# Merging eight masked score levels one at a time in the odd mixer of a two-layer block pair

## What is computed

```python
G = jnp.cumsum(gc, axis=2)
decay = jnp.exp(jnp.where(tri, G[:, :, :, None, :] - G[:, :, None, :, :], -jnp.inf))
scores = jnp.einsum('bhik,bhjk,bhijk->bhij', qc, kc, decay)
o = jnp.einsum('bhij,bhjv->bhiv', scores, vc) + jnp.einsum('bhik,bhkv->bhiv', qc * jnp.exp(G), s)
```

## Time and profile before

| | |
|---|---|
| Median of 3 runs | 3082.21 us (3080.93 to 3082.76) |
| The profiled execution | 3080.94 us, its span 3079.1 us |
| TensorE's share of the span | 97% |
| VectorE's share of the span | 24% |
| The odd mixer's units | about 943 to 1260 us into the span |

### The profile page before, as it was taken

The page is one execution under the profiler, slowest core; times in us unless marked ns, Lnnn a source line. Parts: engine busy times, 40 slices in busy tenths (PEclk is TensorE's granted clock), DMA queues, the critical chain, the costliest instruction groups (busy, mean ns, idle before and its releaser), DMA issues.

```text
span 3079.1 us, 41222 instructions
## 1 busy us (share of the span) xinstructions
PE 2976.5 (97%) x17952; PEld 1702.2 (55%) x17952; DVE 732.1 (24%) x1737; ACT 399.4 (13%) x981; POOL 252.1 (8%) x339
## 2 busy tenths in 40 slices
PE   7999899999999999999999999999999999999998
PEld 3546654444459998667657777454444444444434
DVE  1327722000046665400141001242000000000002
ACT  1114220000022222100031000131000000000001
POOL 2113310000012221200000000000000000000030
PEclk9999999999999999999999999999999999999999
DMA  9860022122122222354335332319999999999993
GB/s 361 320 256 3 15 82 82 60 84 82 57 72 59 76 76 84 117 191 157 122 111 205 143 143 103 127 55 392 361 402 385 385 402 384 384 403 385 384 404 122
DMA packets 214210, 618.59 MB, mean 201 GB/s; under 512 B 6840, under 2 KB 54168, under 8 KB 207504
## 3 DMA queue, kind: packets, MB, share of 16 engines
q1 hardware_dynamic: 206128, 594.30, 50.9%
q0 software_dynamic: 7296, 20.54, 2.0%
q10 hardware_dynamic: 608, 1.12, 0.1%
HBM read 608.67 MB, written 7.26 MB: 200 GB/s over the span
## 4 chain that ended last, share of the span: by engine, by line
PE 91%; DVE 3%; DMA 2%; issue 2%; ACT 1%; PEld 0%; PEldq 0%; POOLq 0%; POOL 0%; DVEq 0%; SPq 0%; ACTq 0%
PE ps_main L677 15%; PE ps_main L719 7%; PE ps_moe_down L3329 6%; PE ps_moe_up L3279 6%; PE ps_moe_gate L3279 6%; PE ps_second L677 6%; PE ps_main L2120 6%; PE ps_lin L1516 4%; PE ps_moe_down L3337 3%; PE ps_moe_gate L3284 3%; PE ps_moe_up L3284 3%; PE ps_second L719 3%; PE ps_main L2143 2%; PE ps_main L564 1%; PE ps_mod L1445 1%
## 5 line engine op out<-in xcount | busy, mean ns | idle before, releaser
L677 PE MATMUL ps_main<-hT,ring_buf 128*128 128x256 f32 (+2 forms) x1408 | 447.9, 479 | 2.4 <-issue 1.6
L677 PEld LDWEIGHTS ps_main<-hT,ring_buf 128*128 128x128 f32 x1408 | 263.7, 190 | 187.0 <-issue 169.2
L719 PE MATMUL ps_main<-ring_buf,ffn_hiddenT 128*128 128x512 f32 x528 | 228.9, 593 | 1.8 <-issue 1.8
L2120 PE MATMUL ps_main<-ring_buf,hT 128*128 128x256 f32 (+1 forms) x992 | 196.1, 352 | 0.3 <-issue 0.3
L677 PE MATMUL ps_second<-hT,ring_buf 128*128 128x256 f32 (+1 forms) x896 | 192.3, 376 | 2.3 <-DMA ring_buf<-in_w_ffn_up_dram 1.0
L3502 DVE TENSOR_TENSOR moe_hidden_buf<-moe_silu_buf,ps_moe_up 128x768 f32<-128x768 f32 (+1 forms) x32 | 27.3, 854 | 664.7 <-PE ps_moe_up L3284 664.7
L677 PEld LDWEIGHTS ps_second<-hT,ring_buf 128*128 128x128 f32 x896 | 167.1, 190 | 28.4 <-issue 5.3
L2120 PEld LDWEIGHTS ps_main<-ring_buf,hT 128*128 128x128 f32 x992 | 166.4, 191 | 17.8 <-issue 0.6
L719 PEld LDWEIGHTS ps_main<-ring_buf,ffn_hiddenT 128*128 128x128 f32 x528 | 99.5, 190 | 127.7 <-issue 127.6
L1516 PE MATMUL ps_lin<-ring_buf,hT 128*128 128x448 f32 (+1 forms) x384 | 133.1, 500 | 1.0 <-ACT hT L1576 1.0
L3279 PE MATMUL ps_moe_up<-ring_buf,moe_xg_buf 128*64 128x512 f32 (+1 forms) x672 | 131.8, 545 | 0.0
(11 more groups left out here) (547 smaller groups left out, 3524.3 us busy)
## 6 DMA issues: line engine op xcount, KB each, us to landing
ring_buf<-in_w_exp_down_dram SPq DMA_DIRECT2D x17, 4096.0 KB, 18.5
ring_buf<-in_w_exp_up_dram SPq DMA_DIRECT2D x16, 4096.0 KB, 18.7
ring_buf<-in_w_exp_gate_dram SPq DMA_DIRECT2D x15, 4096.0 KB, 19.8
mod_pieces<-in_mod_w_dram SPq DMA_DIRECT2D x40, 1024.0 KB, 6.5
moe_third<-in_w_exp_gate_dram SPq DMA_DIRECT2D x9, 4096.0 KB, 19.6
moe_third<-in_w_exp_up_dram SPq DMA_DIRECT2D x8, 4096.0 KB, 19.1
moe_third<-in_w_exp_down_dram SPq DMA_DIRECT2D x7, 4096.0 KB, 18.5
ring_buf<-in_odd_w_in_dram SPq DMA_DIRECT2D x40, 512.0 KB, 6.2
```

Source lines behind the costliest of these rows:

```text
L677: mm = nc.tensor.matmul(ps[:, lo:wide], view[:, k, i * P:(i + 1) * P], hT[:, k, first_col + lo:first_col + wide], start=k == 0, stop=k == ...
L719: mm = nc.tensor.matmul(ps_y[i % 2][:, h, :], hidT[:, b, i * P:(i + 1) * P], view[:, b, h * 512:(h + 1) * 512], start=first, stop=end)
L2120: mm = nc.tensor.matmul(ps[:, 0:width], hT[:, k, t * P:(t + 1) * P], view[:, k, 0:width], start=k == 0, stop=k == KD - 1)
```

## The change

One line sets the number of squares to one and the rounds to eight:

```diff
-            PLACES, ROUNDS = 2, NL // 2
+            PLACES, ROUNDS = 1, NL
             merged = tail(2, 4096, 2 * PLACES * P).rearrange("p (b s n) -> p b s n", b=2, s=PLACES)
```

## The result

The change made the kernel slower by a little: the ratio of the times after to before is 1.0015, with a 95% interval of 1.0009 to 1.0022. That is 4.6 us, between 2.8 and 6.8; the medians of 18 runs each are 3086.36 and 3080.77 us, 5.6 apart, which the interval holds too. Forecast were 4.4 us, and "within 0.2%".

What follows compares the result with a forecast made beforehand. PE bounds the kernel (busy 41.66 of 42.18 us a head), with VectorE's run ending where PE waits; 7 x 0.52 + 0.8 = 4.4 us on a median of 3082.21 gave 3086.5 us, range 3081.5 to 3091.

Steps and rivals of the forecast that it cites:

- The place: At `output(u+1)` (L2152), PE already waited 0.06 us for VectorE's run ending in `take(u)`; no slack there.
- The price of a copy: In VectorE's merges, a predicated copy of 128 columns takes 0.303 us, making a merge 0.80 us longer, 2.55 against 1.75.
- A head: Odd mixer: `output(u+1)` 1.19 us later, less 0.67 saved by the three later outputs, makes a head 0.52 us longer.
- The idle time that vanished: On VectorE ahead of `merge(u+1)`, waiting for its scores: 0.41 us of the first merge's delay goes into it.
- The stall: PE, ready 0.22 us earlier at `output(u+1)`, stands still some 1.5 us once in each of seven heads.
- The last head: Each `scores` waits for the merge ahead of it; less one matmul, this head is 0.8 us longer.
- The sum: Over the mixer, 7 x 0.52 + 0.8 = 4.4 us longer, with nothing later absorbing it.
- The dear copy: Rival in the merges: from 0.318 us a copy the sum passes 6.2 us; at 0.34, 3091 us. Chance 0.15.
- the cheap one: Rival in the merges: copy of 0.222 to 0.290 us, sum -5 to +3 us, 3077 to 3085. Chance 0.15.
- Links don't overlap: Rival in the merges said links overlap: a merge no longer than 1.75 us, PE keeps 7.1 us, 3075. Chance 0.05.
- The granted clock stayed full: Rival said PE's clock falls at each head's new stall: eight losses of 1.7 us, 14 us, 3100. Chance 0.03.
- The skill's rule: For VectorE's merges, a fixed latency per instruction, 0.157 us estimated: a merge grows 0.63 us, the sum about 1.5 us.

Runs made afterwards that it cites:

- the matmul alone: Against the kernel before: merges unchanged, each output takes only the first of two squares; mixer -5.4 us, whole time -1.2 us (-4.3 to +1.8).
- one of 6.6: Changed kernel with a projection moved ahead of the second output, last head keeping two squares; against before, mixer -6.6 us, whole time -12.6 us.
- the eleven kernels: The change and its follow-up variants, each measured against the kernel before; whole-time differences from -12.6 to +11.1 us.

## Why the prediction was right

- **The place.** In the seven heads PE waits for VectorE's merges and takes once a head, at `output(u+1)`, and nowhere else, as written. `output(u+2)` and `output(u+3)` wait for nothing new.
- **The price of a copy.** Expected 0.303 us with slopes at 0.298 and 0.309; measured 0.300. Expected growth of a merge 0.80 us; measured 0.79 for the first and 2.53 - 1.76 = 0.77 for the second.
- **A head.** Expected 0.52 us longer, measured 0.45. The shift of `output(u+1)` was 1.10 where 1.19 was written, and the rest is the three matmuls behind it, which gave back 0.67 as written. Of the missing 0.09, the merges account for 0.04. The idle time that vanished was 0.42 and not 0.41, and the first merge began 0.04 us earlier against PE's own steps. These are the terms of the sum that were off. Behind the wait `take(u+2)` came 1.29 us later where 1.6 was written; it ends at 1049.61 and PE loads `output(u+3)` at 1051.01, so it is covered by 1.4 us, where 1 was expected.
- **The stall.** Expected some 1.5 us without PE, measured 1.38.
- **The last head.** Expected 0.8, measured 0.74. Its last output was to load at 1259.6 in the times of before, 1.0 us later; it came 1.03 later.
- **The sum.** 7 x 0.45 + 0.74 = 3.9 us in the mixer for 4.4 expected; the whole time says 4.6, with an interval that holds both. That the median of 3086.36 lies within 0.2 us of the forecast 3086.5 is luck: the three runs that the forecast started from had a median of 3082.21, and 18 runs have 3080.77; from there the same sum gives 3085.2.
- **The rivals.** The dear copy would have needed 0.318 us, the cheap one 0.290 or less, and 0.300 lies between. Links don't overlap: the seven copies' pitch is (2.31 - 0.300) / 6 = 0.335, the duration and 0.035 again. The granted clock stayed full over the head with the stall. The row shown above has 1.00.
- **The skill's rule.** The section on the TRN2 errata of the Trainium skill's page "VectorE: DVE Perf Modes" gave 0.63 us more for a merge, an estimate; the measured 0.79 is larger. Nearly all of the difference is the links: four more of them at 0.034 us are 0.14. The fixed part itself, 0.15 us by the copies' durations at 256 and 512 columns, agrees with the page's 151 cycles, an estimate of 0.157 us.

The prediction put what a whole time can tell at 6.2 us, and the runs bear that out: an effect of 5.4 us in the mixer (the matmul alone) came out as 1.2 in the whole, and one of 6.6 as 12.6. Over the eleven kernels the signed differences between the two measures have a mean of 0.2 us, but they are 2.3 us in size on average, and for three kernels the mixer's value lies outside the whole time's interval. A part of it goes with the clock: of the 18 runs of the change, the three with a mean granted clock of 0.995 took 3081.2 us on average, the five with 0.992 3087.6. Why the clock differs between runs of one kernel was not studied.

## What to carry to other kernels

VectorE was busy for 63% of a head and still set PE's time, since its work came in one run that ended exactly where PE was waiting. A short saving on the full engine is worth its price only where it isn't followed at once by a wait for another engine. Look for the wait that has none (the load follows the release by 0.08 us), and place other work of the full engine there before making the other engine's part longer. An effect of a tenth of a per cent is read better from marks around the changed stage in one profile, with repeated heads as its own error bar, than from the whole time.

## What the runs showed of the hardware

A predicated copy from PSUM with a mask from SBUF takes 300 ns for 128 columns, 444 for 256 and 737 for 512: nearly a straight line of 1.14 ns a column above a fixed 0.15 us, steeper than the product of the same shapes (287, 423 and 692 ns, 1.05 to 1.06 a column). A link between two of these copies adds 0.034 to 0.035 us at each of these widths; at 512 columns three of them in the even mixer fill 2.28 us, so their starts are (2.28 - 0.737) / 2 = 0.772 apart.
